# A fox/dilated-window decoder layer on one core: first splits interleaved, small broadcasts held back, half gates and batch weight casts re-ordered, sample transposes grouped

## The reference

```
h = rmsnorm(x);  z = h @ w_in          # q,k,v,f for fox; q,k,v for dsw; gates ga, gb
A = forgetting attention, 8 heads x 64 (per-head norm of q,k; cumulative log-sigmoid decay)
B = dilated window attention, 8 heads x 64 (norm + rotary; windows 128/512/2048)
m = sigmoid(ga)*(A @ w_o_fox) + sigmoid(gb)*(B @ w_o_dsw)
x = x + m @ w_out;   x = x + SwiGLU(rmsnorm(x))      # hidden 2816
```

## Time and profile before

| what | value |
|---|---|
| median of 3 runs (lowest, highest) | 1103.33 us (1102.66, 1104.41) |
| the profiled execution's own time | 1102.8 us |
| its span | 1101.1 us |
| mean granted clock of PE, share of full | 0.974 |
| PE busy | 1029.4 us (93%) |
| DVE, ACT, POOL busy | 501.6, 370.8, 103.5 us |
| prompt attention, 224 to 364 us: PE busy | 122.04 of 140 us |
| sample batches, 364 to 584 us: PE busy, DMA share, rate | 197.46 of 220 us, 0.80, 263 GB/s |
| SwiGLU and down projection, 713 to 1101 us: PE busy | 383.26 of 388 us |

### The profile page before, as it was taken

How to read it: one execution, slowest core, us unless ns; L and a number is a source line. 1 busy time by engine, 2 the same in 40 slices (tenths; PEclk the granted TensorE clock), 3 DMA queues, 4 the chain that set the end, 5 groups by cost and what they waited for, 6 DMA issues and landing times.

```text
span 1101.1 us, 22149 instructions
## 1 busy us (share of the span) xinstructions
PE 1029.4 (93%) x9021; PEld 897.8 (82%) x9021; DVE 501.6 (46%) x1032; ACT 370.8 (34%) x669; POOL 103.5 (9%) x173
## 2 busy tenths in 40 slices
PE   3999999979899899888988999999999999999998
PEld 2767774856667666666668999999999999999998
DVE  3245881257665333333335653545455555522221
ACT  7334450345554322333236333322222222312211
POOL 4410010021004311111100000000000000000000
PEclk7999999989999898999899999999999999999999
DMA  7437794433641787887782442232323232033331
GB/s 213 154 125 257 286 356 156 124 118 111 224 181 56 255 273 257 277 272 269 262 262 81 117 121 65 77 96 76 95 78 93 78 93 76 26 106 101 89 100 31
DMA packets 152591, 167.62 MB, mean 152 GB/s; under 512 B 11568, under 2 KB 116416, under 8 KB 151872
## 3 DMA queue, kind: packets, MB, share of 16 engines
q1 hardware_dynamic: 141424, 145.30, 41.0%
q10 hardware_dynamic: 6112, 15.05, 4.0%
q0 software_dynamic: 4976, 6.17, 1.9%
HBM read 159.50 MB, written 40.40 MB: 182 GB/s over the span
## 4 chain that ended last, share of the span: by engine, by line
PE 75%; DVE 9%; ACT 7%; DMA 3%; issue 3%; SPq 0%; POOL 0%; ACTq 0%; DVEq 0%; POOLq 0%
PE bank L1185 38%; PE bank L1230 9%; PE bank L1315 6%; PE bank L1401 4%; PE bank L1507 3%; PE bank L1417 3%; PE bank L1456 2%; ACT buffer L679 2%; DVE buffer L968 2%; DMA buffer<-in_cache_k_fox 2%; ACT w_split L628 1%; DVE wqkv_split L833 1%; DMA buffer<-in_x_prompt 1%; PE bank L1434 1%; PE bank L1287 1%
## 5 line engine op out<-in xcount | busy, mean ns | idle before, releaser
L1185 PE MATMUL bank<-x_split,w_split 128*128 128x272 f32 x2064 | 259.8, 288 | 0.6 <-DVE w_split L941 0.6
L1185 PEld LDWEIGHTS bank<-x_split,w_split 128*128 128x128 f32 x2064 | 259.5, 189 | 0.8 <-DVE w_split L941 0.8
L1230 PE MATMUL bank<-wqkv_split,x_split 128*128 128x512 f32 x576 | 140.5, 401 | 10.8 <-DVE wqkv_split L833 10.8
L1315 PE MATMUL bank<-x_split,w_split 128*128 128x272 f32 x720 | 135.3, 318 | 12.8 <-ACT buffer L659 12.8
L1230 PEld LDWEIGHTS bank<-wqkv_split,x_split 128*128 128x128 f32 x576 | 108.4, 191 | 38.8 <-issue 14.4
L1185 PE MATMUL bank<-h_split,wd_split 128*128 128x272 f32 x1056 | 134.1, 288 | 0.0
L1185 PEld LDWEIGHTS bank<-h_split,wd_split 128*128 128x128 f32 x1056 | 132.8, 188 | 0.1
L1315 PEld LDWEIGHTS bank<-x_split,w_split 128*128 128x128 f32 x720 | 103.6, 199 | 32.7 <-issue 17.9
L941 DVE TENSOR_TENSOR w_split<-buffer,w_split 128x1024 fp32r<-128x1024 f32 x75 | 92.4, 1231 | 81.2 <-ACT w_split L628 78.9
L1401 PE MATMUL bank<-buffer,buffer 128*128 128x128 f32 x416 | 67.9, 292 | 24.0 <-ACT buffer L709 18.4
L628 ACT CAST w_split<-buffer 128x1024 fp32r<-128x1024 f32 x75 | 78.2, 1043 | 35.4 <-PE bank L1185 18.3
(11 more groups left out here) (206 smaller groups left out, 1150.8 us busy)
## 6 DMA issues: line engine op xcount, KB each, us to landing
buffer<-in_cache_k_fox SPq DMA_DIRECT2D x64, 256.0 KB, 3.2
buffer<-in_cache_v_fox SPq DMA_DIRECT2D x64, 256.0 KB, 4.8
buffer<-in_w_in SPq DMA_DIRECT2D x12, 1024.0 KB, 6.3
buffer<-in_w_down SPq DMA_DIRECT2D x16, 704.0 KB, 4.7
buffer<-in_w_gate SPq DMA_DIRECT2D x22, 512.0 KB
buffer<-in_w_up SPq DMA_DIRECT2D x22, 512.0 KB
buffer<-in_state_k_dsw SPq DMA_DIRECT2D x40, 256.0 KB, 4.2
buffer<-in_state_v_dsw SPq DMA_DIRECT2D x40, 256.0 KB, 4.8
```

Source lines behind the costliest of these rows:

```text
L1185: x = mm(banks[hf][:, 0:HALF], w(a, e), src[:, b, k, hf * HALF:(hf + 1) * HALF], start=(first and n == 0 and e == 0), stop=(last and n == ...
L1230: x = mm(bank[t][:, :], x_tile(a, 4 * kh + k, t), WQs[:, kh, b, k, :], start=(kh == 0 and n == 0 and k == 0), stop=(kh == 1 and n == 2 and ...
L1315: x = mm(bank[e][:, 0:HALF], WS[:, s, a, k * 128:(k + 1) * 128], X2[:, b, k, hf * HALF:(hf + 1) * HALF], start=(m % 24 == 0), stop=(m % 24 ...
```

## The change

Six edits. (1) POOL waits for the first w_in tile before its seven small transfers. (2) ACT's square root moves behind the splits; high parts of x^T, x^T copies and the two weight casts are interleaved, with `wq_hi(0)` behind four high parts, and DVE makes `wq_lo(0)` after four low parts and `wq_lo(1)` before the reciprocal; PE's first half waits for only the four k-tiles that it reads. (3) The q/k transposes go round four banks, and the four sample transposes of a block stand together behind the unit with c == 1, copied by DVE in one operation. (4) In the prompt attention a half's gate copy moves from the start of ACT's next step to right behind the exponentials of the step in which the half ends. (5) In a batch ACT's `w_hi` and the copy of key chunk 10 go ahead of `probs_of(b+1, 0)`. (6) Before the batches, `w_hi(GP+1)` moves from behind chunk 4 to behind chunk 8, and `w_lo(GP+1)` from behind chunk 5 to behind chunk 9.

```diff
@@ POOL
+            pool.wait_ge(wq_in[0], 16)
             for n, g in enumerate((kn_f, qn_f, kn_d, qn_d)):
...
             pool.wait_ge(tr_v, 8)
+            pool.wait_ge(trs_ok, 4)
@@ ACT, start (sqrt of ssq was here, then x_hi(0..4), wq_hi(0), x_hi(5..7), x_copy(0..7), wq_hi(1))
+            nc.scalar.copy(X2[:, 0, :, TP:T], xgs).then_inc(xsh_ok, 1)
+            for k in range(4):
+                x_hi(k)
+            wq_hi(0)
+            x_copy(0)
+            x_hi(4)
+            x_copy(1)
+            x_hi(5)
+            x_copy(4)
+            x_hi(6)
+            x_copy(2)
+            x_hi(7)
+            x_copy(3)
+            wq_hi(1)
+            for k in range(5, KT):
+                x_copy(k)
             act.wait_ge(eps_ok, 1)
             act.wait_ge(ss_ok, 5)
             nc.scalar.activation(ssq, ssq, ACT.Sqrt, bias=epsc, scale=1.0 / D).then_inc(std_ok, 1)
@@ ACT, copies of q/k
-                b0 = 2 * (u % 3)
-                nc.scalar.activation(dst[:, 0:TP], bank[b0][:, :], ACT.Copy, scale=sc)
-                nc.scalar.activation(dst[:, TP:T], bank[b0 + 1][:, 0:TS], ACT.Copy, scale=sc).then_inc(tr_a, 1)
+                nc.scalar.activation(dst[:, 0:TP], bank[u % 4][:, :], ACT.Copy, scale=sc).then_inc(tr_a, 1)
@@ ACT, prompt attention
-                if t and half_at(t - 1) != e:
-                    gate(1 + (e - 1) // 2, (e - 1) % 2, 7)
...
                         nc.scalar.activation(PP[n % 3][:, j, 0:N], ..., ACT.Exp, ...).then_inc(p_ok, 1)
+                    if n == NST - 1 or half_at(n + 1) != half_at(n):
+                        e = half_at(n)
+                        gate(1 + e // 2, e % 2, 7)
@@ ACT, batch(b) and the walk before it
                 keys_next(6, 8)
+                w_hi(GP + 2 + b, 1 - s, gates=True)
+                keys_next(10)
                 if not last:
                     probs_of(b + 1, 0)
-                w_hi(GP + 2 + b, 1 - s, gates=True)
-                keys_next(10, 12)
+                keys_next(12)
...
-                if ch == 4:
+                if ch == 8:
                     w_hi(GP + 1, 0)
@@ DVE, start
-            for k in range(KT):
+            for k in range(4):
+                x_lo(k)
             wq_lo(0)
+            for k in range(4, KT):
+                x_lo(k)
+            wq_lo(1)
             dve.wait_ge(std_ok, 1)
...
-            wq_lo(1)
@@ DVE, copies of q/k
+                V.tensor_scalar(dst[:, 0:TP], bank[u % 4][:, :], sc, None, ALU.mult).then_inc(tr_v, 1)
+                if c == 3:
+                    dve.wait_ge(trs_ps, blk + 1)
+                    V.tensor_scalar((kT, qT)[blk % 2][:, 4 * (blk // 2):4 * (blk // 2) + 4, TP:T],
+                                    bank[4 + blk % 2][:, 0:4 * TS]..., sc, None, ALU.mult).then_inc(trs_ok, 1)
@@ DVE, keys of sequence 0
                 if ch == 5:
-                    w_lo(GP + 1, 0)
                     group(0, 0, 0)
                 if ch == 9:
+                    w_lo(GP + 1, 0)
                     group(0, 0, 1)
@@ PE, projection and transposes
-                            pe.wait_ge(xT_sb, t + 1)
-                            pe.wait_ge(xn_ok, 5 if t < 4 else KT + 1)
+                            pe.wait_ge(xT_sb, n + 1)
+                            pe.wait_ge(xn_ok, 5)
+                        if first and kh:
+                            pe.wait_ge(xn_ok, KT + 1)
...
-                if u >= 3:
-                    pe.wait_ge(tr_v if u % 2 == 0 else tr_a, (u - 3) // 2 + 1)
+                if u >= 4:
+                    pe.wait_ge(tr_v if u % 2 else tr_a, (u - 4) // 2 + 1)
                 for t in range(4):
-                    nc.tensor.transpose(bank[b0][...], rows[:, blk, t, ...], ident)
-                nc.tensor.transpose(bank[b0 + 1][:, 0:TS], rows[0:TS, blk, 4, ...], ...).then_inc(tr_ps, 1)
+                    i = nc.tensor.transpose(bank[u % 4][...], rows[:, blk, t, ...], ident)
+                i.then_inc(tr_ps, 1)
+                if c == 1:
+                    if blk >= 2:
+                        pe.wait_ge(trs_ok, blk - 1)
+                    for d in range(4):
+                        i = nc.tensor.transpose(bank[4 + blk % 2][:, d * TS:(d + 1) * TS], rows[0:TS, blk, 4, ...], ...)
+                    i.then_inc(trs_ps, 1)
```

More of the change, by code:

```diff
@@ L266, in program @@
         tr_ps, tr_a, tr_v = sem("qkT_in_psum"), sem("qkT_copied_act"), sem("qkT_copied_dve")
+        trs_ps, trs_ok = sem("sample_qkT_in_psum"), sem("sample_qkT_copied")
         st_k = sem("rows_stored")
@@ L549, in _, with x_hi, x_copy @@
                 nc.scalar.activation(sqx[0:P], xrow[0:P, t, :], ACT.Square, accum_out=ssq[0:P, t:t + 1]).then_inc(ss_ok, 1)
+            act.wait_ge(g_in, 16)
+            act.wait_ge(xs_ok, 1)
+            nc.scalar.copy(X2[:, 0, :, TP:T], xgs).then_inc(xsh_ok, 1)
+            def x_hi(k):
+                act.wait_ge(xT_ps, k + 1)
+                nc.scalar.activation(X2[:, 0, k, 0:TP], bank[k][:, :], ACT.Copy, scale=g1[:, k:k + 1]).then_inc(xh_ok, 1)
+            def x_copy(k):
+                act.wait_ge(xn_ok, k + 2)
+                nc.scalar.copy(xT[:, k, 0:TP], bank[k][:, :]).then_inc(xT_sb, 1)
+            for k in range(4):
[13 more added lines that the diff above has]
+                x_copy(k)
             act.wait_ge(eps_ok, 1)
@@ L552, in _ @@
             nc.scalar.activation(ssq, ssq, ACT.Sqrt, bias=epsc, scale=1.0 / D).then_inc(std_ok, 1)
-            act.wait_ge(g_in, 16)
-            act.wait_ge(xs_ok, 1)
-            nc.scalar.copy(X2[:, 0, :, TP:T], xgs).then_inc(xsh_ok, 1)
-            for k in range(KT):
[L557 to L564, removed]
             act.wait_ge(rst_ok, 1)
@@ L699, in _ @@
                 step(n)
-                if n == NST - 1:
-                    gate(GP - 1, 1, 7)
             act.wait_ge(st_v, 16 * 2)
@@ L841, in _, with x_lo @@
             lo(X2[:, 1, :, TP:T], xgs, X2[:, 0, :, TP:T], xsh_ok, 1, xn_ok)
-            for k in range(KT):
+            def x_lo(k):
                 dve.wait_ge(xh_ok, k + 1)
                 V.scalar_tensor_tensor(X2[:, 1, k, 0:TP], bank[k][:, :], g1[:, k:k + 1], X2[:, 0, k, 0:TP].bitcast(f32), ALU.mult, ALU.subtract).then_inc(xn_ok, 1)
+            for k in range(4):
+                x_lo(k)
             wq_lo = lambda n: lo(WQs[:, n % 2, 1], WQ[:, n % 2], WQs[:, n % 2, 0], wqh_ok, n + 1, wql_ok)
             wq_lo(0)
+            for k in range(4, KT):
+                x_lo(k)
+            wq_lo(1)
             dve.wait_ge(std_ok, 1)
@@ L932, in _ @@
                 dve.wait_ge(tr_ps, u + 1)
-                b0 = 2 * (u % 3)
-                V.tensor_scalar(dst[:, 0:TP], bank[b0][:, :], sc, None, ALU.mult)
-                V.tensor_scalar(dst[:, TP:T], bank[b0 + 1][:, 0:TS], sc, None, ALU.mult).then_inc(tr_v, 1)
+                V.tensor_scalar(dst[:, 0:TP], bank[u % 4][:, :], sc, None, ALU.mult).then_inc(tr_v, 1)
+                if c == 3:
+                    dve.wait_ge(trs_ps, blk + 1)
+                    V.tensor_scalar((kT, qT)[blk % 2][:, 4 * (blk // 2):4 * (blk // 2) + 4, TP:T],
+                                    bank[4 + blk % 2][:, 0:4 * TS].rearrange("p (c n) -> p c n", n=TS), sc, None, ALU.mult).then_inc(trs_ok, 1)
             def w_lo(c, s):
@@ L1300, in _ @@
                     pe.wait_ge(z_used, 30)
-                if u >= 3:
-                    pe.wait_ge(tr_v if u % 2 == 0 else tr_a, (u - 3) // 2 + 1)
+                if u >= 4:
+                    pe.wait_ge(tr_v if u % 2 else tr_a, (u - 4) // 2 + 1)
                 for t in range(4):
-                    nc.tensor.transpose(bank[b0][:, t * 128:(t + 1) * 128], rows[:, blk, t, c * 128:(c + 1) * 128], ident)
-                nc.tensor.transpose(bank[b0 + 1][:, 0:TS], rows[0:TS, blk, 4, c * 128:(c + 1) * 128], ident[0:TS, 0:TS]).then_inc(tr_ps, 1)
+                    i = nc.tensor.transpose(bank[u % 4][:, t * 128:(t + 1) * 128], rows[:, blk, t, c * 128:(c + 1) * 128], ident)
+                i.then_inc(tr_ps, 1)
[3 more added lines that the diff above has]
+                    for d in range(4):
+                        i = nc.tensor.transpose(bank[4 + blk % 2][:, d * TS:(d + 1) * TS], rows[0:TS, blk, 4, d * 128:(d + 1) * 128], ident[0:TS, 0:TS])
+                    i.then_inc(trs_ps, 1)
                 gate0(16 + 2 * u, 18 + 2 * u)
@@ L1309, in _ @@
             pe.wait_ge(tr_v, 8)
+            pe.wait_ge(trs_ok, 4)
             def gate(s, m, e):
```

## The result

The changed kernel takes 1096.21 us (median of 16 runs, 1086.63 to 1102.44) beside 1103.18 us (16 runs, 1100.57 to 1107.5) of the kernel before on the same chip: ratio 0.993, 95% interval 0.9911 to 0.9948. It is faster by 7.0 us, where 15.7 was forecast (1087.6). That is inside the range, but at the time of rival B (1096.8), not of the forecast.

What follows compares the result with a forecast made beforehand. PE, busy 93% of the span, bounds the kernel, so only its waits or low clock can be won. Start 6.6, transposes 1.0, gate copies 1.3, sequence 0 3.7 and batches 3.1 sum to 15.7: 1087.6 us, range 1073 to 1099.

Steps and rivals of the forecast that it cites:

- rival B: Batches: the longer single wait brings the low clock in every batch, +6.1 instead of -3.1, 1096.8 us; chance 0.20.
- the clock of the batches: Batches: half clock behind the key wait in two of six batches, 2.3 us each, 4.6 lost.
- The length of the wait: Batches: PE would wait about 3.4 us for key chunk 3, in one piece.
- The start: Before the projection: earlier loads and re-ordered splits start PE's first matmul sooner; 6.6 us gained, passed to the end.
- Transposes: Query/key transposes: grouping the 16 sample transposes in four groups of four saves 1.0 us, at most 1.8.
- Gate copies: Prompt attention: copies 0.42 us earlier in three places on the chain, 1.3 us gained; the 5.7 us wait stays.
- Keys of sequence 0: Walk before the batches: ACT's wait for a gate weight goes; 5.8 us, limited by the DMA queue to 3.7.
- a key wait of 1.9: Walk over sequence 0: chunk 3 lands at about 375.2 where PE would want it at 373.3.
- The floor of 27.3: Batches: SP's list and the full DMA queue keep each period near 27.3 us; six periods 5.6 less.
- Rival A: Batches: the DMA queue is no floor, so removed waits count fully; 34.8 us gained, to 1068.5; chance 0.13.
- C: Batches: low clock lasts past about 5 us, for most of a batch, making the change slower, 1110 us; chance 0.05.
- D: Start: small transfers are not what delays the loads; gain 4.2 instead of 6.6, 1090.0 us; chance 0.12.

Runs made afterwards that it cites:

- m2: Kernel before plus the start, transpose, gate-copy and batch-order edits, walk over sequence 0 in the old order; 1097.6 us, ratio 0.9922 to the kernel before.
- e3: Changed kernel plus 28 matmuls with unread results ahead of PE's wait for key chunk 3; 1089.1 us, ratio 0.9859 to the kernel before.
- e4: Changed kernel with SP reading the next sequence's eight page numbers early, between fox key loads; 1085.2 us, ratio 0.9823 to the kernel before.
- f1: Changed kernel plus early page numbers (sequence 1's too) and 14 filler matmuls at key chunk 3; 1075.0 us, ratio 0.9735 to the kernel before.
- f2: Changed kernel without the batch and walk re-ordering, plus early page numbers and 14 filler matmuls at key chunk 3; 1104.0 us, ratio 0.9982 to before.
- f4: Kernel before with only the two start edits (small transfers held back, splits re-ordered); 1097.1 us, ratio 0.9933 to the kernel before.
- h3: Kernel before with only POOL's small transfers held behind the first weight tile; 1100.8 us, ratio 0.9965 to the kernel before.
- h4: Kernel before with only the grouped sample transposes; 1101.9 us, ratio 0.9951 to the kernel before.
- e2: Changed kernel without the batch and walk re-ordering, so start, transposes and gate copies alone; 1094.4 us, ratio 0.9891 to the kernel before.
- m1: Kernel before plus start, transpose, gate-copy and walk edits, batches in the old order; 1091.4 us, ratio 0.9846 to the kernel before.
- e1: Kernel before with only the re-ordering of the batches and of the walk over sequence 0; 1108.7 us, ratio 1.0026 to the kernel before.
- h1: Changed kernel without batch and walk re-ordering, plus 18 filler matmuls ahead of PE's wait at key chunk 12; 1088.6 us, ratio 0.9841 to before.

## Why the prediction was wrong, step by step

*The step that failed is the clock of the batches: "I take two of six batches: 4.6".* The count was wrong: half clock came in all six. The price fits: 13.8 us of lost clock over six periods is 2.3 each, as forecast. Without the lost clock the six periods would be 175.3 - 13.8 = 161.5, or 26.9 each, beside the 27.3 forecast as the floor. That subtraction is fair only if lost clock reaches the period in full, and m2, with the same order of the batches, supports it: its one period at full clock is 27.29 long, its five others, at 0.89 to 0.96, are 28.3 to 30.4. Three of the six:

```profile
372.83:401.73 28.90, 24.94 (x357) 19.21 (x349) 10.10 (x31) 8.32 (x17) 5.32 (x9) 0.95 0.79 261
401.73:432.15 30.42, 26.37 (x358) 20.03 (x357) 10.10 (x31) 8.29 (x17) 5.33 (x9) 0.89 0.73 249
461.68:488.97 27.29, 24.01 (x365) 18.26 (x357) 10.10 (x31) 8.40 (x17) 5.34 (x9) 1.00 0.83 276
```

So the miss of the six periods (168.6 forecast, 175.3 measured) is 9.2 of clock, less 2.5 of floor. That covering the wait brings the clock to 1.00 and the time down (after to e3; e4 to f1, where sequence 1's page numbers also come early) shows that the clock is what costs.

*Why the count was wrong.* I had taken it from one trace of the kernel before, and had given rival B 0.20 because of four waits of 2.3 without half clock behind them. More profiled executions say otherwise. Here are six periods of each kernel without additions; f2 is left aside, as its trace is of its slowest execution:

| order of the batches | kernels | periods with half clock | six periods, us | lost clock in them, us |
|---|---|---|---|---|
| old | before, f4, h3, h4, e2, m1 | 3, 4, 5, 5, 6, 6 of 6 | 169.4, 167.0, 167.2, 172.6, 174.6, 168.0 | 8.5, 6.8, 10.2, 13.7, 17.1, 12.0 |
| new | after, e1, m2 | 6, 6, 5 of 6 | 175.3, 177.0, 173.5 | 14.1, 15.4, 10.2 |

(Lost clock is summed here from the clock records themselves; by the rounded windows above it is 13.8 for after.) The old order with its waits of 2.3 had half clock in 29 of 36 periods, the new one in 17 of 18. The trace that I counted in has the fewest such periods of all, and it is not shown that the longer wait is what brings half clock, as B has it. What differs clearly is what a stretch costs. In the old order 14 of 18 periods with one short stretch (1.7 us lost) are 27.6 to 28.0 long, no longer than the seven periods at full clock (27.4 to 28.4). In the new order the eleven periods with a short stretch are 28.3 to 30.5, beside 27.3 at full clock. So the re-ordering made the batches a little shorter at full clock, by the one such period there is, and took away what had hidden the stretches; why they are hidden in the one order and not in the other is not shown. e4 and f2 show that early keys, or a filler at another place, do not end half clock while PE's wait stays uncovered.

The length of the wait was priced from the longest of five waits for keys (1.32 at 490.72, of 3.8 us in all; the first of them, 0.39, is at 440.73, not where the earlier trace rows has it); measured were 3.4 at the longest and 2.9 on average. The Trainium skill ("TensorE: Matmul & The Clock Gate", section "Why this matters for your kernels") had the rule that longer idle gaps of PE send it back to half rate; after agrees, with waits of up to 3.4 and half clock in six of six periods. The waits of 2.3 in e2 and m1, also followed by it in six of six, are shorter gaps, of which that rule does not speak, and the trace of before, with no longer ones in the batches, could not test it.

*The start, 6.6.* Right in mechanism and somewhat small: 7.8 at the first matmul, 8.2 at the projection's end. The cast started at 14.02 where I had 14.8.

*Transposes, 1.0.* The mechanism was right, the size was not: 3.4 (h4). I priced a small transpose at its own 0.24; on the path it cost 0.38, the difference between units with and without one. From the full transposes to the small one 0.53 passed; without one the next gate matmul follows 0.35 behind them (200.45 to 200.80). The distances to its neighbours, and not the small one's own length, were its price.

*Gate copies, 1.3.* 1.1 in the profiles, the 5.8 us wait still there, as said.

*Keys of sequence 0, 3.7.* Wrong: -0.1. ACT's wait for w_in went, as forecast, but PE then stood 3.35 for key chunk 3 and ran at half clock behind it, in a stretch that I had costed at a key wait of 1.9 (375.2 less 373.3) and at full clock. m1, where the batches are left alone, shows 1.6 for it beside e2, and 1.0 beside before.

*The floor of 27.3.* A floor of this order of issue only. e4's six periods were 27.6 on average at 273 GB/s, its shortest 26.1, and f1's 25.9 at 291, where before moved 267. Rival A was right that the queue was not full, wrong that the change would use it.

*Rivals.* B is what came in its count and its time; its reason, the longer wait, is not shown, as said above. C did not come: no batch was at half clock for more than 6.8 of its 29 us. But two of the six stretches were that long, past the "5 us or so seen so far", and so were two in the kernel before (from 426.3 and from 538.9), which I had not read to their ends. D fell with h3.

The errors were of both signs: +3.8 in the front, -3.8 in the walk, -6.5 in the batches. With the same prices and six cold batches of six, the sum would have been 15.7 - 9.2 = 6.5 us. That this is near the 7.0 measured is in part luck, as the errors of front and walk cancel.

## What to carry to other kernels

Before taking away a wait, ask which wait takes its place and what it had hidden: here a wait of 2.3 gave way to one of 2.9 on average at another place, PE's work did not change, and stretches of lower clock that the old order had mostly absorbed now reached the time. Count such stretches in several executions before giving them a chance. A wait that can't be removed is cheaper covered with matmuls, but only at the place where PE really stands; at any other they are added work. And where transfers are late, look first for what the issuing engine does between its issues: eight page numbers read at another place were worth more than the whole change.

## What the runs showed of the hardware

- The same wait of 2.3 us is followed by half clock in some executions and periods and not in others: in three of six periods of the kernel before, in four to six of six in five other kernels with that wait. One trace is too few to set a chance from. Runs of the changed kernel spread with it: span times (1 - granted clock of the whole span) is 16 us in its fastest run (1086.6 us, 0.985) and 33 in its two slowest (1102.3 and 1102.4, 0.970).
- A period's length doesn't follow its clock alone: m1 has a period of 27.6 at a clock of 0.94, h1 one of 27.3 at 1.00, and in the new order m2 has 27.3 at 1.00 and 28.9 at 0.95.
- A lone 32x32 transpose between full ones costs 0.38 us on PE's path; four together cost 0.57.
- Reading eight page numbers held SP for 4.8 us (401.90 to 406.74, after; with the reading elsewhere, in f1, the gap between the same two issues is 0.2), longer than issuing the eight loads of values behind it (4.14).
